# Strassen feed-forward: VectorE's side work placed by unit in the down parts, weight rests ahead of weight sums, two first halves first, modulations one per step

## What is computed

```
mix = concat([o_gla, o_lru, o_mla]) @ w_out
x = _layer_norm(DEEPNORM_ALPHA * x + gate1 * mix, ln1_g, ln1_b)
h2 = x * (1 + scale2) + shift2
g_ff, u_ff = jnp.split(h2 @ ffn_w_gu, 2, axis=-1)
f = (jax.nn.silu(g_ff) * u_ff) @ ffn_w_down
x = _layer_norm(DEEPNORM_ALPHA * x + gate2 * f, ln2_g, ln2_b)
```

## Time and profile before

| | us |
|---|---|
| median of three runs | 3627.26 |
| lowest and highest | 3620.04, 3630.15 |
| the profiled execution | 3621.66 |
| its span, first to last instruction | 3619.9 |
| PE busy (share of the span) | 3291.5 (91%) |
| DVE busy | 2348.2 (65%) |
| ACT busy | 1579.6 (44%) |

### The profile page before, as it was taken

One profiled execution on the slowest core, in us unless ns is written; L12 is line 12 of the kernel. 1 busy time (PEld: TensorE's weight loads), 2 busy tenths in 40 slices (PEclk: granted clock), 3 DMA queues, 4 the chain that ended last, 5 costly groups with the idle time before them and its releaser, 6 DMA issues. The chain is left out here.

```text
span 3619.9 us, 61473 instructions
## 1 busy us (share of the span) xinstructions
PE 3291.5 (91%) x23676; PEld 2765.7 (76%) x23676; DVE 2348.2 (65%) x4510; ACT 1579.6 (44%) x3163; POOL 193.8 (5%) x252
## 2 busy tenths in 40 slices
PE   6988898998999998999979868989989899999997
PEld 5864556776988888999869535666769898899996
DVE  5135665445488889878742366644446888888887
ACT  5235454444254454444332445544433454543432
POOL 0011210110000000000000121111100000000000
PEclk9997999998999999999989969999999999999998
DMA  5144002443033232222111500034411233322231
GB/s 209 32 142 155 26 1 94 163 153 104 13 110 93 88 95 79 85 81 84 48 52 30 194 29 1 1 142 159 167 47 58 82 99 89 91 82 79 88 105 52
DMA packets 157573, 316.91 MB, mean 88 GB/s; under 512 B 18491, under 2 KB 85341, under 8 KB 146406
## 3 DMA queue, kind: packets, MB, share of 16 engines
q1 hardware_dynamic: 145766, 229.08, 20.4%
q0 software_dynamic: 11520, 83.89, 6.5%
HBM read 306.41 MB, written 6.51 MB: 86 GB/s over the span
## 5 line engine op out<-in xcount | busy, mean ns | idle before, releaser
L2383 ACT CAST w_ffn_hi<-w_ffn 128x512 fp32r<-128x512 f32 x616 | 366.8, 617 | 283.8 <-DVE w_ffn L2562 192.9
L437 PE MATMUL psum<-h_lo,w_ffn_hi 128*128 128x256 f32 (+1 forms) x1408 | 407.6, 290 | 0.0
L436 PE MATMUL psum<-ffn_act_hi,w_down_hi 128*128 128x288 f32 (+1 forms) x992 | 341.5, 344 | 63.9 <-DVE w_down_lo L2580 56.7
L2574 DVE TENSOR_TENSOR w_ffn_lo<-w_ffn,w_ffn_hi 128x1024 fp32r<-128x1024 f32 (+1 forms) x366 | 383.9, 1049 | 15.6 <-ACT w_ffn_hi L2383 15.3
L436 PE MATMUL psum<-h_forms_hi,w_ffn_hi 128*128 128x288 f32 x1232 | 365.1, 296 | 3.9 <-DVE w_ffn_lo L2574 3.4
L436 PE MATMUL psum<-h_hi,w_ffn_hi 128*128 128x256 f32 x1232 | 348.7, 283 | 18.9 <-DVE w_ffn_lo L2574 17.1
L438 PE MATMUL psum<-h_forms_hi,w_ffn_lo 128*128 128x288 f32 x1232 | 364.3, 296 | 0.0
L438 PE MATMUL psum<-h_hi,w_ffn_lo 128*128 128x256 f32 x1232 | 347.1, 282 | 0.0
L438 PE MATMUL psum<-ffn_act_hi,w_down_lo 128*128 128x288 f32 (+1 forms) x992 | 333.4, 336 | 0.0
L437 PE MATMUL psum<-ffn_act_lo,w_down_hi 128*128 128x288 f32 (+1 forms) x992 | 333.2, 336 | 0.0
L422 DVE SCALAR_TENSOR_TENSOR xT<-psum,adaT,xT 128x512 f32<-128x512 f32 (+3 forms) x432 | 235.0, 568 | 142.2 <-PE psum L438 142.0
(11 more groups left out here) (443 smaller groups left out, 7608.8 us busy)
## 6 DMA issues: line engine op xcount, KB each, us to landing
w_ffn<-in_w_gu SPq DMA_DIRECT2D x352, 256.0 KB, 2.6
w_ada_pair<-in_w_ada SPq DMA_DIRECT2D x40, 1024.0 KB, 5.2
w_down<-in_w_down SPq DMA_DIRECT2D x192, 192.0 KB, 2.4
w_ada_first<-in_w_ada SPq DMA_DIRECT2D x4, 2048.0 KB, 21.7
w_out<-in_w_out SPq DMA_DIRECT2D x16, 512.0 KB, 7.4
w_in_T<-in_w_in_T SPq DMA_DIRECT2D x12, 512.0 KB, 4.4
w_down<-in_w_down SPq DMA_DIRECT2D x48, 128.0 KB, 2.1
z<-in_x_prompt SPq DMA_DIRECT2D x8, 512.0 KB, 6.9
```

Of the source, the lines that this page charges most:

```text
L436: pe.matmul(o, wh, xh, start=first, stop=False)
L437: pe.matmul(o, wh, xl, start=False, stop=False)
L2383: act.copy(WGH[:, (j + 1) % NR].bitcast(F32R), WGR[:, m % 2, i]).then_inc(s_wh, 1)
L2574: dve.tensor_tensor(WGL[:, m % 2, i:i + n].bitcast(F32R), WGR[:, m % 2, i:i + n], WGH[:, r:r + n], ALU.subtract).then_inc(s_wl, n)
```

## The change

- `down_units`: in parts 8 to 14 the first four units are c = 0 and 1 with the first token half, then c = 0 and 1 with the second; before they were c = 0 to 3 with the first half. So PE asks for the second half's activation rest at unit 2 and no longer at unit 4, and the blocks c = 0, 1, 2 are complete after units 2, 3 and 5 (before 4, 5 and 6).
- `beside` and `BESIDE`: what DVE does beside the residuals hangs on the number of the unit. First half: rests of c = 5, 6, 7 after units 2, 3, 4; statistics after 3; sums after 4; scales after 5; leading weight rests after 5, 6, 7. Second half: rests after units 5, 7, 8; statistics after 3; scales or rows after 9; sums after 10; weight rests after 11, 13, 15.
- ACT rounds c = 5, 6 and 7 first and then does the roots and the row blocks.
- In `step` the weight rests come ahead of the sums, and the sums are split: 1 and 3 at i = 1, 2 and 4 at i = 2.
- The eight modulations come one per step, i = 1 to 4 of two pairs.

```diff
--- before.py
+++ after.py
@@ -364,10 +364,10 @@
                 affine(eng, XT[:, c, t0:t0 + w], back_psum(g, c)[:, 0:w], PRM[:, g_col + c:g_col + c + 1],
                        PRM[:, b_col + c:b_col + c + 1]).then_inc(xt[par], 1)
 
-            def modulate(eng, par, g, t0, t1):
+            def modulate(eng, par, g, t0, t1, one=None):
                 eng.wait_ge(tb, KD * (g + 1))
                 eng.wait_ge(xt[par], 4 * g + 4)
-                for k in range(par, KD, 2):
+                for k in range(par, KD, 2) if one is None else (par + 2 * one,):
                     affine(eng, HT[:, k, t0:t1], XT[:, k, t0:t1], ADA[:, sc + k, 0:1],
                            ADA[:, sh + k, 0:1]).then_inc(md[par], 1)
 
@@ -2120,10 +2120,11 @@
             if q < NQ // 2:
                 return [(c, (0, 512), 4 + c % 4) for c in range(KD)]
             if q < NQ - 1:
-                return [(u % 4 if u < KD else u // 2, HALVES[1][u // 4 if u < KD else u % 2], 4 + u % 4)
-                        for u in range(2 * KD)]
+                first = [(0, 0), (1, 0), (0, 1), (1, 1)] + [(u // 2, u % 2) for u in range(4, 2 * KD)]
+                return [(c, HALVES[1][h], 4 + u % 4) for u, (c, h) in enumerate(first)]
             return [(c, LG_SPAN[1], 4 + c % 4) for c in range(KD)] + [(c, LG_SPAN[2], c % 4) for c in range(KD)]
 
+        BESIDE = [((2, 3, 4), 3, 5, 4, (5, 6, 7)), ((5, 7, 8), 3, 9, 10, (11, 13, 15))]
         DONE = [{c: u + 1 for u, (c, _, _) in enumerate(down_units(q))} for q in range(NQ)]
 
         def stage_out_ffn():
@@ -2295,6 +2296,8 @@
                         norms_beside(q)
                         pe.wait_ge(s_ul, 2 * m1 - 1 if q >= QH else 2 * m1)
                         for u in range(first):
+                            if u == 2:
+                                pe.wait_ge(s_ul, 2 * m1)
                             part(u, last).then_inc(s_dn, 1)
                         for u in range(first, len(units)):
                             c = units[u][0]
@@ -2302,8 +2305,6 @@
                             bank_free(u)
                             for f in range(last):
                                 part(u, f)
-                            if u == first:
-                                pe.wait_ge(s_ul, 2 * m1)
                             part(u, last).then_inc(s_dn, 1)
                             if q == NQ - 1 and u == KD + 1:
                                 turn2(pe, 4)
@@ -2375,7 +2376,7 @@
                         if i in (0, 4, 5):
                             act.wait_ge(s_set[m % 2], 64 * (m // 2 + 1))
                         else:
-                            act.wait_ge(s_ws, 4 * m + {3: 1, 2: 2, 1: 3, 6: 4}[i])
+                            act.wait_ge(s_ws, 4 * m + {3: 1, 1: 2, 2: 3, 6: 4}[i])
                         if j >= NR:
                             act.wait_ge(s_pp, j - NR + 1)
                         else:
@@ -2445,10 +2446,12 @@
                             act.activation(U2T[:, 0:w], U2T[:, 0:w], ACT.Silu).then_inc(s_sb, 1)
                             if m == m1 - 1:
                                 act_rounded(m, 1)
-                        if m == PAIRS[QH - 1][0] and i in (1, 4):
-                            mod1(act, i // 4, 2, TB0, TP)
-                        if not final and m == PAIRS[QH + 6][0] and i in (1, 4):
-                            mod2(act, i // 4, 0, 0, 512)
+                        r = 4 * (m - PAIRS[QH - 1][0]) + i - 1
+                        if PAIRS[QH - 1][0] <= m < PAIRS[QH - 1][0] + 2 and 1 <= i <= 4:
+                            mod1(act, r // 4, 2, TB0, TP, r % 4)
+                        r = 4 * (m - PAIRS[QH + 6][0]) + i - 1
+                        if not final and PAIRS[QH + 6][0] <= m < PAIRS[QH + 6][0] + 2 and 1 <= i <= 4:
+                            mod2(act, r // 4, 0, 0, 512, r % 4)
                     for k in range(KD):
                         act.copy(MXH[:, k].bitcast(F32R), HT[:, k]).then_inc(s_xh, 1)
                         if final and k == 0:
@@ -2483,11 +2486,10 @@
                             for p in range(3):
                                 form_rounded(1, p)
                         for c in range(NW, KD if q < NQ - 1 else NW):
-                            if c == KD - 1:
-                                norms_beside(q, 1)
                             down_rounded(q, c)
                             if q == QH - 1:
                                 form_rounded(1, c - 2)
+                        norms_beside(q, 1)
                         norms_beside(q, 2)
                         if q == QH - 1:
                             form_rounded(1, 6)
@@ -2561,7 +2563,7 @@
                             dve.wait_ge(s_ws, 4 * m + 1)
                             ins = dve.tensor_tensor(w[:, 1], w[:, 3], w[:, 0], ALU.subtract)
                         if p == 4:
-                            dve.wait_ge(s_ws, 4 * m + 3)
+                            dve.wait_ge(s_ws, 4 * m + 2)
                             ins = dve.tensor_tensor(w[:, 6], w[:, 4], w[:, 1], ALU.subtract)
                         ins.then_inc(s_ws, 1)
 
@@ -2604,13 +2606,13 @@
                         dve.tensor_tensor(UR[:, m - PAIRS[PART[m]][0], w:2 * w], U2T[:, 0:w], C22T[:, 0:w],
                                           ALU.mult).then_inc(s_um, 1)
 
-                    def norms_beside(q, c):
-                        if c == 1:
+                    def norms_beside(q, first):
+                        if first:
                             for blk in LN1_AT.get(q, ()):
                                 stats1(dve, lk2, blk)
                             for blk in rows2.get(q, ()):
                                 stats2(dve, lk2, blk)
-                        if c == 4:
+                        else:
                             for blk in LN1_AT.get(q, ()):
                                 scale1(dve, lk2, blk)
                             for blk in rows2.get(q, ()):
@@ -2652,11 +2654,11 @@
                         if i == 6:
                             dve.wait_ge(s_c22, m + 1)
                             dve.tensor_tensor(u2, p, u2, ALU.add).then_inc(s_c12, 1)
-                        if i == 2 and m + 1 < NPAIR and not (m == m0 and q - 1 in SUMS_IN_D):
-                            for n in range(1, 5):
-                                w_sum(m + 1, n)
                         for g in LO_AT[j]:
                             w_rest(*g)
+                        if i in (1, 2) and m + 1 < NPAIR and not (m == m0 and q - 1 in SUMS_IN_D):
+                            for n in ((1, 3), (2, 4))[i - 1]:
+                                w_sum(m + 1, n)
                         if i == 5:
                             dve.wait_ge(s_sa, m + 1)
                             dve.wait_ge(s_c21, m + 1)
@@ -2675,6 +2677,21 @@
                         if m == PAIRS[QH - 1][0] + 1 and i == 3:
                             samples1(dve)
 
+                    def beside(q, u, b):
+                        for c in range(NW, KD):
+                            if u == b[0][c - NW]:
+                                down_rest(q, c)
+                        if u == b[1]:
+                            norms_beside(q, True)
+                        if u == b[2]:
+                            norms_beside(q, False)
+                        if u == b[3] and q in SUMS_IN_D:
+                            for n in (1, 3, 2, 4):
+                                w_sum(PAIRS[q][1] + 1, n)
+                        if u in b[4]:
+                            for g in LO_D[q][b[4].index(u):b[4].index(u) + 1]:
+                                w_rest(*g)
+
                     def down(q):
                         if q == 0:
                             kept1(dve, 0)
@@ -2691,17 +2708,8 @@
                             if q and q != NQ // 2:
                                 dve.wait_ge(s_dv, U0[q - 1] + (u + 1 if q < NQ - 1 else DONE[q - 1][c]))
                             residual(dve, lk2, s_dv, TMPF, bank(b), c, span, M_G2)
-                            if q < NQ - 1 and u + 1 == DONE[q][c]:
-                                norms_beside(q, c)
-                                late = int(q >= QH)
-                                if 2 + late <= c <= 4 + late:
-                                    down_rest(q, c + 3 - late)
-                                if c == 3 - late and q in SUMS_IN_D:
-                                    for n in range(1, 5):
-                                        w_sum(PAIRS[q][1] + 1, n)
-                                if c >= 5:
-                                    for g in LO_D[q][c - 5:c - 4]:
-                                        w_rest(*g)
+                            if q < NQ - 1:
+                                beside(q, u, BESIDE[q >= QH])
                             if q == NQ // 2 - 1 and u == 0:
                                 h_sum(1, 3)
                             if q == NQ // 2 - 1 and u >= 1:
@@ -2750,7 +2758,7 @@
```

(2 more changed lines are left out.)

## The result

| | before | after |
|---|---|---|
| median of four runs, us | 3628.68 | 3573.16 |
| lowest and highest | 3620.04, 3630.15 | 3564.7, 3576.81 |
| profiled execution, us | 3621.66 | 3573.69 |
| its span | 3619.9 | 3571.9 |
| stage of the first layer | 802.8 | 776.4 |

The ratio is 0.985, 95% interval 0.9825 to 0.9872: 1.5% faster. 3566 was predicted, and 3548 to 3598 as the range.

What follows compares the result with a forecast made beforehand. PE was taken as the bound, with DVE's order deciding when it waits. Second halves 32.9, first halves 11.6 and products 18.0, less 6.8 for clock, gave 55.7 us: 3621.66 to 3566, range 3548 to 3598.

Steps and rivals of the forecast that it cites:

- rival (a): The forecast itself: 3566 us, own range 3556 to 3576; chance 0.58.
- second halves, down parts and transposes, with clock: Parts 8 to 14: 26.2 us waits, 15.3 half clock, 2 refilling removed; 3.5 and 7.1 added; net 32.9 faster.
- first halves without part 7, waits and clock: Parts 0 to 6: net 11.6 us faster from waits and clock, less 6.8 for new half clock.
- part 7's down part: Last first-half part: no sums there, order kept on both engines, so its 2.2 us of waits per layer stay.
- products: Strassen products: of 20.5 us weight-rest waits 16.2 go, plus 1.8 of refilling; net 18.0 faster.
- Unit 2: Second-half down parts: PE waits 0.28 us for the second activation rest, about 0.28 net per part, 3.5 in all.
- Unit 15: Second halves: late residual, 1.25 us in four second-layer parts, about 1.05 in part 14 of both layers; together 7.1.
- walk of part 1: First-half part 1: new waits of 0.6 us at unit 7 and 3.75 at the next part's first product; gains nothing.
- The clock: Added first-half waits may bring half clock: 0 to 1.7 us in each of four parts, taken as 6.8.
- part 1's row: Waits of 1.38 and 2.44 us there kept clock 1.00; by it the sum is 6.8 better, 3558.
- product 6 of pair 5: PE's 1.42 us wait: the rest comes 1.2 us earlier, near 1082.8, where PE wants 1082.7.
- waits inside pair 21: Part 7: modulations one at a time, so the waits of 0.7 and 1.0 us at pair 21 go.

## Why the prediction was right, and where its terms were not

The forecast was 55.7 us of gain for the profiled execution; the profiled pair has 48.0, the time is 3573.7 and not 3566. The medians differ by 55.5, but that they meet the forecast so well is luck: the profiled execution before is 7 us under its median, the one after is at its median, and the kernel before had medians of 3618.8 to 3621.5 beside the other runs. The time lies in the own range of rival (a), and the mechanism was the one walked. By terms, in lost time, where measured values sum to 47.4 with rounding:

| term | predicted | measured |
|---|---|---|
| second halves, down parts and transposes, with clock | -32.9 | -29.4 |
| first halves without part 7, waits and clock | -4.8 | -9.2 |
| part 7's down part | 0 | +3.1 |
| products | -18.0 | -12.0 |

**Second halves.** All waits for rests of the down weights are gone and so are all nine pieces at half clock. Unit 2 costs 0.27 in parts 8 to 11 as said; in parts 12, 13 and 15 of the second layer it shows 0.73 to 0.82, but there unit 4 had waited 0.46 to 0.59 for its bank before, so the net is again near 0.27. Unit 15 waits 1.54 in the four parts, not 1.25, and 1.17 and 1.43 in part 14, not 1.05: 8.8 us for 7.1, and none in the first layer's parts 8 to 11, as said. The nine pieces had cost 12.9 us and not 15.3. What the prediction had not was 2.7 us at the transposes. They now wait for the reading of the last product: 0.33 in parts 9 and 11, where product 6 had waited about as long for its rest before, a wait that moved by a few instructions and that I had counted as gone; and 1.42 and 1.06 in part 8, before 1.01 and 0.3.

**First halves.** The walk of part 1 gave 0.6 at unit 7 and 3.75 at the next first product; the rows show 0.56 and 3.42 (in lost time 0.60 to 0.73 and 3.59 to 3.62), and after part 4 1.84 to 1.88 where 1.75 was said. The experiment with early scales confirms the cause, since one number in the order takes these waits away. The term came out 4.4 better. What was removed, waits with refilling and clock, was 35.8 us and not 32.7; what was added was 26.7 and not 27.9.

**The clock.** 3.75 us of idle were taken to cost 1.7 in each of four places, against the reading by part 1's row that they might cost nothing. (By that reading the sum is 6.8 better, 3559; the prediction has 3558.) All four pieces are there. Each costs 1.5 us and not 1.7, which was half of 3.41: at half clock matmuls of 256 columns start 0.213 us apart and not twice 0.120, here in the piece behind part 1.

```profile
1110.01 0.42 PE L437 MATMUL psum<-h_forms_a_lo,w_ffn_hi 128*128 128x256 f32 x1
1110.22 0.42 PE L438 MATMUL psum<-h_hi,w_ffn_lo 128*128 128x256 f32 x1
```

The Trainium skill (TensorE: Matmul & The Clock Gate, section "HAM oscillation") has long idle gaps bring the half-rate clock back each time; for the gaps of 3.4 us the traces agree, four of four. On shorter ones the traces alone speak: of 18 idle times between 2.06 and 2.44 us in the kernel before, 12 had a piece at half clock in or behind them and 6 had none.

**Products: the step that was mis-sized.** 16.2 us of waits were to go with 1.8 of refilling, and waits for `w_ffn_lo` were to fall from 20.5 us to some 4; the list shows 10.0. The waits of product 6 of pair 5 behaved nearly as walked, and pair 1's first wait stayed at 1.5 per layer. Three things failed. The waits inside pair 21 were said to go and remained, 1.19 and 0.85 at product 2 and 0.6 at product 6. The split brought new ones, 0.9 at pair 2 and 1.3 at pair 23 in each layer, 4.4 us in all. And 0.37 is left at product 6 of pairs 5 and 11. I had walked DVE around the operation that was moved forward and not around those that it was moved past; the result, "the waits go", was walked at pair 5 and taken over for parts 3, 7 and 8.

**Part 7** was said to keep its order. Its down order is kept, but with two sums later in the last pair DVE enters the down part late: unit 0 waits 0.62 for the last activation rest, which is new, and unit 4's wait grew by 0.2, in each layer. The second layer also has a piece at half clock behind unit 5's wait of 2.20 us that the same wait did not bring before; these 1.6 us are not shown to come from the edit.

**Which part did it.** Alone, the side work gives 34.9, the order of units 16.1, the split 5.6 and the modulations 3.0, together 59.6; the whole gave 47.4. The four can't simply be added, and the pieces at half clock are the larger part of the reason: by them alone the four runs save some 32 us together and the whole 10. The side work and the order of units also shorten the same wait at unit 10. What is shown is that the side work by unit alone carries most of the change, that it takes away the waits for the rests of the down weights, and that with it in place the order of units adds nothing that can be measured and the split some 4 us.

## What to carry to other kernels

Here DVE, 78 to 86% busy in the parts read above, decided by its order how long PE waits. So look first for such an engine's own idle holes and put long work that nobody waits for into them, and let a short operation that another engine waits for go ahead of long ones that are not wanted yet. When an operation is moved, walk also what it is moved past: the wait that you removed is often standing three instructions further on. If an order hangs on an event (a block that is finished), changing the event moves everything that hangs on it, and an experiment has to hold these apart. And count the pieces at half clock before a difference of a few microseconds between two profiles is put down to an edit.
